# The last u pair of a gated conv and retention decoder layer as a half-size-product unit

## The reference, cut to what matters

```
proj = rms_norm(x) @ w_in         # split: a_val, a_gate, q, k, v, g, gate_a, gate_b
u = a_val * sigmoid(a_gate)       # 512 channels
conv = causal depthwise conv, 31 taps, over u (and cached rows for the samples)
a_out = silu(layer_norm(conv)) @ w_conv_out
o = retention(rotary(q), rotary(k), v);  b_out = (silu(g) * norm(o)) @ w_ret_out
m = (sigmoid(gate_a) * a_out + sigmoid(gate_b) * b_out) @ w_o
h = x + rms_norm(m);  y = h + rms_norm(relu(rms_norm(h) @ w_up)**2 @ w_down)
```

## Time and profile before

| | us |
|---|---|
| median of 3 runs | 1496.62 (1496.47 to 1496.68) |
| the profiled execution's own time | 1496.33 |
| span of the profile, first to last instruction | 1494.5 |
| TensorE busy | 1473.9 (99%) |
| VectorE busy | 1001.5 (67%) |
| GpSimd busy | 844.1 (56%) |
| ScalarE busy | 636.2 (43%) |

### The profile page before, as it was taken

One profiled execution on the slowest core, in us unless ns is written; L12 is line 12 of the kernel. 1 busy time (PEld: TensorE's weight loads), 2 busy tenths in 40 slices (PEclk: granted clock), 3 DMA queues, 4 the chain that ended last, 5 costly groups with the idle time before them and its releaser, 6 DMA issues.

```text
span 1494.5 us, 28310 instructions
## 1 busy us (share of the span) xinstructions
PE 1473.9 (99%) x11336; PEld 1454.4 (97%) x11336; DVE 1001.5 (67%) x1252; ACT 636.2 (43%) x930; POOL 844.1 (56%) x571
## 2 busy tenths in 40 slices
PE   8999999999999999999999999999999999999996
PEld 5999999999999999999999999999999999999995
DVE  7999888866545724576715876766757765574847
ACT  5533443344544541131213855556556332332333
POOL 3377776777545652257565445555555655554555
PEclk9999999999999999999999999999999999999998
DMA  6013333321356258621321144566759575454634
GB/s 217 22 42 94 113 115 110 115 82 65 112 171 212 74 197 300 218 80 50 146 78 53 29 146 174 199 233 218 255 199 326 203 286 187 143 209 155 227 107 170
DMA packets 110091, 229.13 MB, mean 153 GB/s; under 512 B 8960, under 2 KB 20992, under 8 KB 108304
## 3 DMA queue, kind: packets, MB, share of 16 engines
q1 hardware_dynamic: 95296, 204.30, 39.3%
q10 hardware_dynamic: 14672, 23.09, 4.6%
HBM read 154.41 MB, written 72.95 MB: 152 GB/s over the span
## 4 chain that ended last, share of the span: by engine, by line
PE 96%; POOL 1%; DVE 1%; issue 1%; ACT 1%; DMA 0%; POOLq 0%; SPq 0%; DVEq 0%; ACTq 0%
PE ps L1478 40%; PE ps L1239 26%; PE ps L1028 16%; PE ps L1404 3%; PE ps L1391 3%; PE ps L1076 1%; PE ps L1166 1%; PE ps L1171 1%; PE ps L1182 1%; PE ps L1168 1%; PE ps L1149 0%; PE ps L1154 0%; PE ps L1196 0%; POOL w_l L933 0%; DVE xn_l L2280 0%
## 5 line engine op out<-in xcount | busy, mean ns | idle before, releaser
L1478 PE MATMUL ps<-tx_l,w_h 128*128 128x258 f32 x960 | 271.3, 283 | 0.0
L1478 PE MATMUL ps<-tx_h,w_h 128*128 128x258 f32 x960 | 271.3, 283 | 0.0
L1478 PE MATMUL ps<-tx_h,w_l 128*128 128x258 f32 x960 | 271.1, 282 | 0.0
L998 POOL TENSOR_TENSOR w_l<-raw,w_h 128x512 fp32r<-128x512 f32 x120 | 186.2, 1555 | 146.7 <-ACT w_h L2037 146.3
L1478 PE MATMUL ps<-fx_l,w_h 128*128 128x258 f32 x720 | 203.7, 283 | 0.0
L1478 PE MATMUL ps<-fx_h,w_h 128*128 128x258 f32 x720 | 203.4, 283 | 0.0
L1478 PE MATMUL ps<-fx_h,w_l 128*128 128x258 f32 x720 | 203.4, 282 | 0.0
L1478 PEld LDWEIGHTS ps<-tx_h,w_h 128*128 128x128 f32 x960 | 181.4, 189 | 0.0
L1478 PEld LDWEIGHTS ps<-tx_l,w_h 128*128 128x128 f32 x960 | 181.3, 189 | 0.0
L1478 PEld LDWEIGHTS ps<-tx_h,w_l 128*128 128x128 f32 x960 | 181.2, 189 | 0.0
L2336 DVE SCALAR_TENSOR_TENSOR ps<-u_ext,wdw,ps 128x512 f32<-128x512 f32 x232 | 155.2, 748 | 0.0
(11 more groups left out here) (390 smaller groups left out, 4307.2 us busy)
## 6 DMA issues: line engine op xcount, KB each, us to landing
raw<-wseq_dram SPq DMA_DIRECT2D x260, 256.0 KB, 3.0
quad_scratch<-quad_h SPq DMA_DIRECT2D x16, 774.0 KB, 3.6
tx_h<-quad_scratch SPq DMA_DIRECT2D x12, 1032.0 KB, 10.1
tx_l<-hidden_scratch SPq DMA_DIRECT2D x12, 1032.0 KB, 12.7
gate_scratch<-gst SPq DMA_DIRECT2D x10, 1032.0 KB, 4.9
hidden_scratch<-hq_g SPq DMA_DIRECT2D x8, 1032.0 KB, 6.9
hidden_scratch<-stg_b SPq DMA_DIRECT2D x6, 1032.0 KB, 6.9
hq_g<-hidden_scratch SPq DMA_DIRECT2D x6, 1032.0 KB, 13.0
```

Of the source, the lines that this page charges most:

```text
L998: pool.tensor_tensor(lo, src, hi.bitcast(F32), ALU.subtract).then_inc(q_lo, 1)
L1478: out = pe.matmul(ps[:, 2 * n + s, 0:HC], RINGS[q % RING][wa][:, kk * P:(kk + 1) * P], OPS[x][xb][:, QK * kh + kk, at_:at_ + HC], start=(i ...
```

## The change: what it does

The pair of groups `G_U + 6` and `G_U + 7` goes. Its columns (slots 12 to 15 of the weight stream, which keeps its order) become unit 0 of XU = 21 units, `X_U`; all others move up by one unit, with their tables. So the direct phase has 12 slots, and the first unit begins after group `G_U + 5`. In the u unit the rows of the gate get their sigmoid on ScalarE out of "e2" and "e7", and VectorE multiplies them in two instructions of 128 x 516 at the start of unit 1 (`u_unit_out`), followed by `u_sample(3)`.

The eight half sums of x are split: GpSimd makes the first four (two after each of slots 8 and 9), VectorE the last four (`second_sum`). VectorE's order before the first unit becomes: taps(10), u_out(1), u_sample(1), four half sums, low parts of operands 2, 3 and 4, taps(2), u_out(2), u_sample(2), low part of operand 5. The tap counts in the units change: 5 + 5 in unit 0, 4 + 1 + 5 in unit 1, 5 + 1 + 6 in units 2 to 5, 5 + 6 in units 6 to 9 (before: 4 + 1 + 5 in units 0 to 3, 4 + 1 + 6 in unit 4, 5 + 6 in 5 to 8). On ScalarE the high part of operand 5 goes ahead of the third high part of the first unit's weights. As the number of units is odd now, the last product shares a bank with the first chunk of the first output group; that group's first eight matmuls write the two other chunks.

The diff, cut to its core (left out are the tables and constants that move by one unit or four slots):

```diff
@@ -72,23 +72,26 @@
 
 G_XSTAT = 0
 G_U, S_U = 1, 0
-XU = 20
+XU = 21
 OFF = 4 * XU
-G_AOUT, S_AOUT = 9, 16
+G_AOUT, S_AOUT = 7, 12
 EARLY = KT - 2
-G_BO0, S_BO0 = 17, 24
+G_BO0, S_BO0 = 15, 20
 G_BOH, S_BOH = G_BO0 + EARLY, S_BO0 + EARLY
 G_BO1, S_BO1 = G_BOH + 2, S_BOH + 4
-G_WO, S_WO = 31, 40
-G_WOB, S_WOB = 35, 48
-G_FFN, S_FFN = 41, 56
+G_WO, S_WO = 29, 36
+G_WOB, S_WOB = 33, 44
+G_FFN, S_FFN = 39, 52
 S_FAST = S_FFN + 4 * DIRECT
 
 
-X_G, X_GA, X_GB = (0, 1, 2, 3), (4, 5, 6, 7), (8, 13, 14, 17)
-X_KQ, X_V = ((9, 10), (15, 16)), ((11, 12), (18, 19))
+X_U = 0
+X_G, X_GA, X_GB = (1, 2, 3, 4), (5, 6, 7, 8), (9, 14, 15, 18)
+X_KQ, X_V = ((10, 11), (16, 17)), ((12, 13), (19, 20))
 X_GATES = X_G + X_GA + X_GB
-X_RET = 13
+X_RET = 14
+U_SLOTS = 12
+OPERAND_AT = {2: 1, 3: 2, 4: 3, 5: 4}
 RET_A = {1: 0, 3: 1, 6: 2, 8: 3, 11: 4, 13: 5, 16: 6, 18: 7}
 RET_B = {2: 0, 4: 1, 7: 2, 9: 3, 12: 4, 14: 5, 17: 6, 19: 7}
 DEC_LOAD = {1: 0, 4: 1, 7: 2, 10: 3, 14: 4, 17: 5, 21: 6, 24: 7}
...
@@ -885,15 +890,9 @@
                 f11, f12, f21, f22, f5 = x_sums(half)
                 if n == 0:
                     pool.tensor_tensor(f5, f12, f11, ALU.subtract).then_inc(xs_sum, 1)
-                elif n == 1:
+                else:
                     pool.wait_ge(xs_sum, half + 1)
                     pool.tensor_tensor(f12, f22, f12, ALU.subtract).then_inc(xs_sum, 1)
-                elif n == 2:
-                    pool.wait_ge(xs_sum, half + 3)
-                    pool.tensor_tensor(f22, f22, f5, ALU.subtract).then_inc(xs_sum, 1)
-                else:
-                    pool.wait_ge(xs_sum, half + 5)
-                    pool.tensor_tensor(f21, f21, f22, ALU.subtract).then_inc(xs_sum, 1)
 
             def unit_sum(v, n):
 
@@ -914,15 +913,14 @@
                     pool.wait_ge(xw_lo, STEPS * v + 4)
                     pool.tensor_tensor(wx_y[:], raw[:, 1, :], raw[:, 2, :], ALU.subtract).then_inc(xw_op, 1)
 
-            for n in range(RAW, 16):
-                if n == 15:
-                    unit_sum(0, 0)
+            for n in range(RAW, U_SLOTS):
                 low_part(n % RAW, n)
                 if n == 2 * RAW:
                     pool.wait_ge(xs_sc, KT)
-                    x_sum(0)
-                if 2 * RAW <= n < 15:
-                    x_sum(n - 2 * RAW + 1)
+                if 2 * RAW <= n < 2 * RAW + 2:
+                    x_sum(2 * (n - 2 * RAW))
+                    x_sum(2 * (n - 2 * RAW) + 1)
+            unit_sum(0, 0)
 
             def unit_low(v, k):
 
@@ -1117,9 +1115,8 @@
                         out = second_mms(t, c, half)
                         if c == CHUNKS - 1:
                             out.then_inc(mm, 1)
-            with pe.Fori(0, CT - 2) as i:
-                group8(G_U + 4, S_U + 8, XN, i, i * 4)
-                group8(G_U + 5, S_U + 10, XN, i, i * 4)
+            group8(G_U + 4, S_U + 8, XN)
+            group8(G_U + 5, S_U + 10, XN)
 
             def taps_done():
 
@@ -1204,7 +1201,7 @@
             def unit_bank(v, k):
 
                 if v == 0 and k < 2:
-                    taken(pe, G_U + 6 + k)
+                    taken(pe, G_U + 4 + k)
                 elif k == 0:
                     x_evicted(pe, v - 1, "e5")
                 elif k == 1:
@@ -1231,7 +1228,7 @@
                 n = (a, b, c, a, c, a, a)[i]
                 pe.wait_ge(xw_lo, q + 1)
                 if v == 0 and 2 <= i <= 5:
-                    pe.wait_ge(xs_lo, i - 1)
+                    pe.wait_ge(xs_lo, OPERAND_AT[i])
                 unit_bank(v, k)
                 for s in range(2):
                     for kk in range(QK):
@@ -1289,19 +1286,28 @@
             for c in range(NRC):
                 g, slot = G_AOUT + c, S_AOUT + c
                 if c < 2:
-                    x_evicted(pe, XU - 1, ("e2", "e7")[c])
-                    x_evicted(pe, XU - 1, "e5")
+                    x_evicted(pe, XU - 1, ("e5", "e2")[c])
                 free_set(pe, g)
                 pe.wait_ge(w_split, slot + 1)
                 if c == 0:
-                    for n, sub in enumerate((2, 3, 0, 1)):
+                    for n, sub in ((0, 2), (1, 3)):
+                        pe.wait_ge(piece_ld[sub], CV_LD + 16)
+                        for a in range(2):
+                            for b in (1, 2):
+                                pe.matmul(pch(g, b), W[a][:, slot % HL, sub * P:(sub + 1) * P],
+                                          cva_h[:, sub, b * CH:(b + 1) * CH], start=(n == 0 and a == 0), stop=False)
+                    x_evicted(pe, XU - 1, "e7")
+                    for n, sub in ((0, 2), (1, 3)):
+                        for a in range(2):
+                            pe.matmul(pch(g, 0), W[a][:, slot % HL, sub * P:(sub + 1) * P],
+                                      cva_h[:, sub, 0:CH], start=(n == 0 and a == 0), stop=False)
+                    for n, sub in ((2, 0), (3, 1)):
                         pe.wait_ge(piece_ld[sub], CV_LD + 16)
                         for a in range(2):
                             for b in range(CHUNKS):
                                 pe.matmul(pch(g, b), W[a][:, slot % HL, sub * P:(sub + 1) * P],
-                                          cva_h[:, sub, b * CH:(b + 1) * CH], start=(n == 0 and a == 0), stop=False)
+                                          cva_h[:, sub, b * CH:(b + 1) * CH], start=False, stop=False)
                         if n == 2:
-                            x_evicted(pe, XU - 1, "e7")
                             pe.wait_ge(on_n, 6)
                             pe.wait_ge(rope_done, 8)
                             v_decode(1)
@@ -1587,7 +1593,7 @@
             def x_operand_hi(i):
 
                 if i == 5:
-                    act.wait_ge(mm, done(15))
+                    act.wait_ge(mm, done(U_SLOTS - 1))
                     act.activation(xn_h[:, 0:QK, HALVES[1]], sx_5[:], ACT.Copy).then_inc(xs_hi, 1)
                     return
                 act.wait_ge(xs_sum, 2 * i)
@@ -1626,15 +1632,10 @@
                     weight_hi(9)
             weight_hi(10)
             x_operand_hi(2)
+            u_gate(2)
             weight_hi(11)
-            u_gate(2)
-            weight_hi(12)
             x_operand_hi(3)
-            weight_hi(13)
-            weight_hi(14)
             x_operand_hi(4)
-            u_gate(3)
-            weight_hi(15)
 
             def unit_high(v, k):
 
...
@@ -1768,7 +1769,7 @@
 
                 x = turn(v, j)
                 y = x + 7 * (X_RET - X_KQ[0][0])
-                if (v, j) == (1, 0):
+                if (v, j) == (2, 0):
                     act.wait_ge(h_done, 2 * CT)
                     act.dma_start(convp, u_ext[:, :, SEQ:SEQ + HIST]).then_inc(cv_out, 16)
                     act.dma_start(convs, hist[:]).then_inc(cv_out, 16)
@@ -1827,9 +1828,11 @@
                 if v in X_GATES and X_GATES.index(v) > 1:
                     gate_stored(act, X_GATES[X_GATES.index(v) - 2])
                 if v == 0:
-                    taken(act, G_U + 7)
+                    taken(act, G_U + 5)
                 if v == 1:
                     act.wait_ge(xs_lo, 4)
+                if v == 2:
+                    act.wait_ge(h_done, 2 * CT - 1)
                 if v in X_KQ[1]:
                     gate_stored(act, X_GB[1 + X_KQ[1].index(v)])
                 if v == X_GB[3]:
@@ -1865,13 +1868,16 @@
                 if v in X_GATES and v != X_GB[3]:
                     x_evicted(act, v, "e2")
                     sig_rows(v, 0, 1)
+                if v == X_U:
+                    x_evicted(act, v, "e2")
+                    act.activation(x_row(v, 0), x_row(v, 0), ACT.Sigmoid).then_inc(xg_sg, 1)
                 unit_turn(v, 3)
                 unit_high(v + 1, 0)
                 unit_turn(v, 4)
                 unit_high(v + 1, 1)
                 unit_turn(v, 5)
                 act.wait_ge(xw_pm, x_done(v, 6))
-                if v in X_GA + X_GB[:3]:
+                if v in (X_U,) + X_GA + X_GB[:3]:
                     act.activation(two(x_row(v, 1)), pair(a), ACT.Sigmoid).then_inc(xe_a, 1)
                 else:
                     act.activation(two(x_row(v, 1)), pair(a), ACT.Copy).then_inc(xe_a, 1)
@@ -1880,8 +1886,8 @@
 
             unit_high(0, 0)
             unit_high(0, 1)
+            x_operand_hi(5)
             unit_high(0, 2)
-            x_operand_hi(5)
             for v in range(XU):
                 unit_out(v)
 
@@ -2373,9 +2379,21 @@
                 dve.tensor_scalar(conv[:, j, SEQ:T], conv[:, j, SEQ:T], vec[:, V_BDW + j:V_BDW + j + 1], None,
                                   ALU.add).then_inc(h_done, 1)
 
+            def second_sum(n, half):
+
+                ks = slice(2 * half, 2 * half + 2)
+                f21, f22 = (x_in[:, QK + 2 * half:QK + 2 * half + 2, HALVES[t]] for t in range(2))
+                if n == 2:
+                    if half == 0:
+                        dve.wait_ge(xs_sum, 4)
```

(75 more changed lines are left out.)

32 lines of the change are left out of this document (16 added, 16 removed).

## The result

The changed kernel takes 1504.45 us (median of 5 runs, 1503.45 to 1505.1) against 1496.47 (5 runs, 1496.43 to 1496.68): a ratio of 1.0052, 95% interval 1.004 to 1.0063. It is 8.0 us slower; 1501.8 was predicted. The profiled execution took 1504.17 us with a span of 1502.3, which is 7.8 more than the span of before. Two single executions lie far outside everything else, one of e4 (3192 us) and one of the kernel before that was run beside e9 (3667 us); no ratio uses them.

The account below looks back on a forecast made before the run. TensorE, busy 99% of the span, was taken as the bound: its stream plus holes. -2.53 - 0.54 + 4.6 + 3.7 = +5.2 us on the profiled execution gives 1501.5, and 1501.8 as median; range 1494.6 to 1505.0.

Parts of the forecast that it names:

- rival 4: TensorE's granted clock falls behind the first unit's hole; one product at half clock adds 2.9 us: 1504.7; chance 0.10.
- Products -2.53: On TensorE, a unit of 20.20 us replaces the last u pair's direct matmuls of 22.73 us: 2.53 us gained.
- first unit's old loss -0.54: The old first unit's fourth product started at 115.48 instead of 114.94 us; that 0.54 us could also go.
- The hole at product 1: First unit: `u_out(2)`, delayed by GpSimd's turns in VectorE's queue, frees the bank late; product 1 starts 4.6 us late.
- units 2 to 5, 3.7 us through "e6": A fifth tap delays the gate products, GpSimd gets in between, and that eviction is late: four units at 0.9 to 1.05 us.
- rival 2: Not slower: VectorE wins the port over waiting GpSimd; hole 1.1 to 2.3 us, nothing lost in units 2 to 5: 1495.1; chance 0.12.
- What was put at 0: Unit 1's start (at most 1 us), cache stores, sigmoid, gate stores, rope steps, weight loads and the x stage's end: no cost.
- The estimate of the hole without it (9.7): Before the first unit: if moving the four sums gained nothing, they take 4 x 2.42 us and the hole is 9.7 us.

Follow-up runs that it names:

- e4: Changed kernel with the fifth tap of units 2 to 5 moved behind the gate products, still 12 taps there: 1499.5 us, ratio 1.0018.
- e9: e7 without the three taps between two evictions of the u unit, one tap more in each of units 2 to 5 behind the gate products: 1494.23 us, ratio 0.9984.
- e1: Changed kernel with the two taps behind `u_out(2)` instead of in front of it: 1501.19 us, ratio 1.0033.
- e6: Changed kernel with the last four half sums of x back on GpSimd, two after each of slots 8 to 11: 1507.78 us, ratio 1.0075.
- e7: e3 with operand 5's low part ahead of operand 4's, `u_out(2)` earlier, `u_sample(2)` at the u unit's end, early taps rearranged: 1497.09 us, ratio 1.0003.
- e8: Changed kernel with one of the two taps ahead of `u_out(2)` and one behind it: 1502.8 us in one run.
- e2: Changed kernel with operand 4's low part behind `u_out(2)` and both taps behind operand 5's low part: 1501.0 us, ratio 1.0029.
- e5: Changed kernel with the edits of e2 and e3 together: 1496.59 us, ratio 1.0 against the kernel before.
- e3: Changed kernel with eleven taps again in units 2 to 5 and the missing ones in units 6 to 9: 1500.12 us, ratio 1.0022.

## Why the prediction was right and wrong

The direction and the place were right, and 1504.45 lies in the range, just under its upper end (1505.0); the size, +5.2 us, was 2.8 short of the 8.0 measured. Two steps failed, the clock (3) and the way in which the taps cost time in units 2 to 5 (4). That the second left no mark on the total, and that rival 4's figure (1504.7) lies so near to the time, is luck.

1. **Products -2.53, first unit's old loss -0.54: right.** e9 shows them: with the new losses taken away 2.1 us of gain is left.
2. **The hole at product 1, 4.6 us: right in place, cause and nearly in size (4.08).** `u_out(2)` ended at 90.6, 91.1 was said. GpSimd took 4.0 us out of VectorE's queue where 4.8 was said. e1 shows that the taps ahead of it count in full: 2.7 us of taps moved, 2.6 of hole gone.
3. **The first failed step: the clock behind the hole was left out of the sum.** It was rival 4, at 0.10, because the stretch behind the idle start showed 1.00. That row was misread: it has 8 matmuls in 4.00 us. The same kind of matmul in the kernel before, in 2 us there and in 2 us a little later (columns as in the earlier trace rows; behind the comma TensorE's busy time and, in brackets, its matmuls: 4 and 8):

```profile
6.00:8.00 2.00, 2.00 (x4) 1.15 (x4) 0.88 (x1) 1.09 (x2) 0.00 (x0) 1.00 1.07 388
```

```profile
12.00:14.00 2.00, 2.00 (x8) 1.33 (x7) 1.59 (x2) 1.35 (x1) 0.82 (x1) 1.00 1.06 377
```

They start 0.57 us apart from 6.38 to 9.82 us and 0.29 apart from 10.30 on. The trace's record of the clock begins at 10.20 us, and the view gives 1.00 where it has no record. In all eleven profiles the distance halves where the record begins (8.7 to 12.0 us). So behind the idle start TensorE ran at half speed, and the row spoke for rival 4 and not against it. (Both kernels begin so, and it hardly reaches the time: the later the clock rises, the less TensorE waits for the sigmoid at 38 us. In the change and all experiments but e6 the first unit begins between 83.45 and 83.81 us.) Rival 4's price was put at 2.9 (a product at half speed); it is 1.5 to 1.7, and 2.1 in e6. In the profiled executions the clock fell for holes of 2.24, 2.77, 4.08 and 6.46 us (e7, e8, the change, e6) and not for those of 1.46, 1.69 and 1.81 (e1, e2, e5). The Trainium skill (TensorE: Matmul & The Clock Gate, "Why this matters for your kernels") says that idle gaps between bursts can bring the lower clock back; the trace agrees (0.67 over the 5 us behind the hole of 4.08), and rival 4 in the mechanism, not in its price, came true beside the forecast.
4. **The second failed step: units 2 to 5, 3.7 us through "e6"; 4.1 measured, of which 1.0 through "e6" and 3.1 through a weight load.** In unit 2 GpSimd arrived 142.73 - 135.74 = 6.99 us after "e2" and VectorE at 7.20, as said (6.96 and 7.2), and "e6" came 0.98 us late. But the delay did not carry on through VectorE. The prediction had put the gate stores at 0, as they "keep their place relative to their units". Their place in SP's queue is ahead of the fourth slot's load, and they wait for the gate products, which it had itself moved by a tap. The products of unit 2 ended 11.6 us after "e2" in place of 8.2; the store and the load followed them, GpSimd waited 4.2 us for the load (4.81 us), and weights were 1.33 us late in unit 3. In units 3 to 5 GpSimd reached the port 0.23 to 0.28 us after VectorE (165.88, 165.60) and the pair passed in 2.37, as rival 2 had it. GpSimd's low part took 3.25, and this cost nothing, since GpSimd still waited for the load behind it (1.47 us at 173.31). Here the tap alone made the store 1.32 us later, and TensorE lost 0.35 to 0.73 us in each of units 4 to 6, whose weights were late. e3 and e4 fit: with the pair 5.87 us after "e2" again, nearly all of the holes go, whether 11 or 12 taps are in the unit. That the load is what is late is read from the chain and the waits; no run takes the store from in front of it.
5. **What was put at 0: the start of unit 1, the cache stores, the sigmoid, rope steps, the direct slots' loads** show no wait in the units. The end of the x stage was put at 0 and shows 0.4 in this profile, by the loads of `cva_h` and not by the bank; in e1 to e7 and e9, with the same end of the stage, it isn't there.
6. **The Trainium skill's remark that moving work between the two engines might not help** (Perfetto Trace Analysis, "Optimizing Scalar/DVE Operations") was given no chance, with the reason that a sum holds VectorE for 1.15 us and GpSimd for 2.42. e6 bears this out: 3.3 us are gained by the move, so here the trace does not agree with the remark. The estimate of the hole without it (9.7) was too large: 6.46 at one place and 1.17 at another.

What is open: whether the length of the hole alone decides on the clock (the lengths above are one execution each, and e7's times suggest that the hole of 2.24 us was not always followed by a fall), how much of the 3.1 us a store behind the load would save, and the 0.4 us that is not placed.

## What to carry to other kernels

When a queue is moved earlier against a fixed consumer, write down both engines of the shared port in order of arrival: the instruction that frees a bank goes first, work on PSUM banks (here the taps) goes where the other engine holds the port, and filler goes behind the evictions that a product waits for. Then follow the late instruction through the queues that only start transfers: a store that waits for it holds up every load behind it. The change itself was worth its 2.5 us; three places in the order of VectorE's work decided between +8.0 and -2.6. A hole in a dense stream of matmuls can cost more than its length (here 1.5 to 1.7 us more behind those of 2.24 to 4.08 us), and that part is looked for in the distance of starts first, since no wait shows it and a granted clock of 1.00 can mean that there is no record.

## What the runs showed of the hardware that was not expected

- **A waiting GpSimd instruction got in between two low parts of VectorE, and not between two gate products.** VectorE's two gate products ran in 2.37 us although GpSimd had been waiting since 0.28 us after their start (GpSimd: 3.25 us for 1.29), and so in units 4 and 5. With GpSimd first by 0.21 us (142.73, 142.94) the pair took 4.41, and a second instruction of GpSimd (144.52) got in between its halves. Among the low parts (80.28 and 83.42) GpSimd got in each time: 3.36 and 3.33 us for 1.3, and VectorE 3.21 and 3.40 for 2.30. The Trainium skill (SBUF — State Buffer, "Who interferes with whom") says that a VectorE instruction with two SBUF inputs contends with a GpSimd instruction that reads SBUF, and that the order of issue decides who blocks; the trace agrees for single instructions. Who gets the gap between two instructions of the other is what these rows add, and they do not settle what decides it.
- **The clock did not fall at once, and once it fell before the hole had ended.** After the 4.08 us hole the first eight matmuls start 0.12 to 0.19 us apart, then sixteen 0.215 apart (91.80 to 95.03), then 0.12 again. Behind the 6.46 us hole of e6 there are about twenty (91.62 to 95.71). In e3, with the same hole (86.5 to 90.57), the granted clock is already 0.50 from 90.20 to 90.50, where no matmul runs; in e6 the matmuls are slow from the second one on.
